# High and low parts of the samples' input rows stacked on 40 partitions: one broadcast product per sample in place of two

## The chip, the cores and the metric

The kernel runs on one core of one Trainium2 chip. The metric is the device time of one execution, in microseconds; lower is better. The comparison is between this kernel and the same kernel with the change.

## What is computed

The reference is one step of a hybrid decoder layer: an adaLN-modulated RMS norm, one input projection, a sliding-window attention branch (A), a gated linear recurrence (B, HGRN2), two merged output projections and a residual. It is done for a prompt of 2048 rows and, apart from that, for one token of each of eight samples. The change touches only one step of the samples' branch B, the update and the reading of the recurrent state (DEC_SEQ is 1, so the chunked scan has one step):

```
# per sample b and head h; S is 128 x 128 (key dim x value dim)
S_new = exp(log_f)[:, None] * S + k_in[:, None] * v[None, :]
o     = q @ S_new
```

Here v is the sample's row of the projection that the kernel calls ib, 4 heads x 128 = 512 values. The outputs are S_new of all samples and, through o, the samples' rows of y.

## The kernel before

**Tiles and stages.** The prompt is worked off in four iterations (`it` 0 to 3) of 512 rows. Each iteration is a fixed list of units (`UNITS`, NU in all): input projections of kinds B, A, za, f, qb, ib, zb, the merge gates ga and gb, the projections pa and pb, and at the end the output units `("o0", t)` and `("o1", t)` for the four row tiles. A unit is up to 24 dense products on TensorE (L717 or L720) into one of two PSUM banks, D0 and D1, which alternate. fp32 operands are split into a high part of type fp32r and a low part, and each product is done as hi x hi, hi x lo and lo x hi. ScalarE makes the high part of weights (L926) and GpSimd the low part (L1580); of the inputs h they are L942 and L1588.

**Order.** Every engine runs through the same list of units and half units, written out in Python. Small side tasks are put between the halves by the table `SIDE`, the samples' work among them. Nothing is scheduled at run time: each engine works in its own order and waits on counting semaphores. `do()` on VectorE makes an instruction increment a semaphore and then waits for it (`settle`); `s.done()` only increments. A unit can start on TensorE when its bank was emptied. For output units VectorE empties the bank in `evac` (L1310) and then adds the residual (L1312); a unit uses the bank of the unit two before it.

**The samples' states.** At the end of iteration 0, ahead of the evacuation of unit NU-3 (an output unit), VectorE runs a set-up block (L1551 to L1558). It waits for `h_lo` and `s_win`, then writes the selector `esel`, in which row b is one in the 128 columns of sample b, splits the eight rows `ibS` into `ib_hi` and `ib_lo`, signals `s_ib`, clears R3 and copies the samples' q into it, and signals `esel`. The semaphore wait on `h_lo` is there because R3 was a buffer of h.

In iteration 1 the task `vB` of sample b follows half unit (b + 1, 0). TensorE broadcasts the sample's row of 512 values to all 128 partitions of bank XD, by two products with the selector as weights:

```
mm(bank[:, :], esel[:, a, :], ib_hi, start=True, stop=False)
ins = mm(bank[:, :], esel[:, a, :], ib_lo, start=False, stop=True)
```

These are L812 and L813. GpSimd has meanwhile scaled the state (L1636), which came by DMA at the start of iteration 1, and VectorE adds the outer product from the bank, head by head (L1517). One unit later the task `so` on TensorE sums q over the new state (L818, four products per sample, one per head, and as many weight loads), which needs L1517 of that sample; the state then goes out by DMA.

Of the kernel before, what the change touches and what calls it, by code (L numbers as in the profile page):

```python
# [11 lines left out]
F32, F32R, I32, U8 = mybir.dt.float32, mybir.dt.float32r, mybir.dt.int32, mybir.dt.uint8  # L12
ALU, ACT, AX = mybir.AluOpType, mybir.ActivationFunctionType, mybir.AxisListType

D, SEQ, NS = 1024, 2048, 8
TB, NIT = 512, 4
P, KT, NT = 128, D // 128, TB // 128
# [281 lines left out]
def build(nc, A, O):  # L299

    ctx = ExitStack()
    with ctx:
        def sb(name, shape, dt=F32):
            return ctx.enter_context(nc.sbuf_tensor(name, shape, dt))


        ident, ones = sb("ident", [P, P]), sb("ones", [P, P])
# [40 lines left out]
        esel_t = sb("esel_t", [P, 1024], F32R)  # L348
# [13 lines left out]
        first = ExitStack()  # L362
        rowsS = first.enter_context(nc.sbuf_tensor("rowsS", [8, 1280], F32))
        first.close()
        rowsR = sb("rows_r", [8, 1280], F32R)
        qkS, vS, ibS = rowsS[:, 0:640], rowsS[:, 640:768], rowsS[:, 768:1280]
        ckv = R3[:, :].rearrange("p (a b n) -> p a b n", a=2, b=4)
        kTs = R2[:, 0:512].rearrange("p (b n) -> p b n", b=4)
        ps_s = kst[0:8]
        AT32 = kst[:, :, :].rearrange("p h (t i) -> p (h t) i", t=NT)  # L370
        sq_in = ibS[:, 0:256]
        esel = esel_t[0:8, :].rearrange("p (b n) -> p b n", b=NS)
        ib_hi, ib_lo = rowsR[:, 0:512], rowsR[:, 768:1280]
        qz_b = R3[:, :].rearrange("p (h b c) -> p h b c", h=HB, b=NS)
        vrow, selbc = kst[0:NV, 0], kst[:, 1]

# [22 lines left out]
        def f32(ap):  # L399
            return ap.bitcast(F32)  # L400
# [245 lines left out]
        def _(pe):  # L646
            mm, tr = nc.tensor.matmul, nc.tensor.transpose
            s = Eng(pe, "none", S)
            s.wait_ge("p_load0", 64)
            for k in range(KT):  # L650
                ins = tr(XA[:, 9 * k:9 * k + 9], R2[0:9, P * k:P * k + P], ident[0:9, 0:9])
            s.done(ins, "p_T")
            s.wait_ge("p_c", 1)
            for p in range(4):
                for k in (2 * p, 2 * p + 1):
                    s.wait_ge(f"ada{k}", 16)
                for n, b in enumerate(("D0", "D1", "XC", "XD")):
                    for k in (2 * p, 2 * p + 1):
                        r = slice(32 * (k % 4), 32 * (k % 4) + 32)
                        ins = mm(pb[b][r, :], cT[:, k, :], ada[k][:, 512 * n:512 * n + 512], start=k < 4, stop=k >= 4)  # L660
# [20 lines left out]
            for n in range(2 * KT):  # L681
                ins = mm(pb["D0"][:, 9 * n:9 * n + 9], mod_rows[:, P * n:P * n + P], sel, start=True, stop=True)
# [41 lines left out]
            def side(it, task, a, key):  # L724
# [8 lines left out]
                b = BANK[key]  # L733
                bank = pb[b]
                if PARTS[key][0] == (task, a):
                    s.wait_ge(f"{b}_free", USE[key])
                if task == "gm":
                    for p in range(4):
                        s.wait_ge(f"gw{p}", 16)
                        for n in range(2):  # L740
                            for k in (2 * p, 2 * p + 1):
                                r = slice(32 * (k % 4), 32 * (k % 4) + 32)
                                ins = mm(bank[r, 512 * n:512 * n + 512], cT[:, k, :],
                                         gate_w[p][:, k % 2, 512 * n:512 * n + 512], start=k < 4, stop=k >= 4)
                elif task == "gb":
                    s.wait_ge("grow", 1)
                    s.wait_ge("p_late", 1)
                    for n in range(2):
                        ins = mm(bank[:, 512 * n:512 * n + 512], selbc, grow[:, 512 * n:512 * n + 512],
                                 start=True, stop=True)  # L750
                elif task == "gS":
                    for k in range(KT):
                        ins = mm(bank[:, NS * k:NS * k + NS], grow[:, P * k:P * k + P], sel[:, 0:NS],
                                 start=True, stop=True)
                elif task == "bu":
                    n = it * NB + a
                    s.wait_ge("p_scale", 1)
                    s.wait_ge(f"w_in{n % NRAW}", came[n])
                    c = [b_ for _, b_ in PARTS[key]].index(a)
                    raw = w_raw[:, n % NRAW]  # L760
                    kind = BLOCKS[a][0]
                    if kind == "pa":
                        s.wait_ge("s_yb", 1)
                        s.freed(0, "sO", 1)
                        for h in range(2):
                            for k in range(4):
                                ins = mm(bank[32 * k:32 * k + 32, P * (2 * c + h):P * (2 * c + h) + P],  # L767
                                         yS[:, 4 * h + k, :], raw[:, 4 * h + k, :], start=True, stop=True)
                    else:
                        if kind == "out":  # L770
                            s.wait_ge("s_y", 4)
                        for k in range(KT):
                            ins = mm(bank[32 * (k % 4):32 * (k % 4) + 32, P * c:P * c + P], hS[:, k, :], raw[:, k, :],
                                     start=k < 4, stop=k >= 4)
# [3 lines left out]
                elif task in ("sx", "sy"):  # L778
# [4 lines left out]
                    else:  # L783
                        for c in range(nb):
                            ins = mm(bank[:, NS * c:NS * c + NS], srow[:, P * c:P * c + P], sel[:, 0:NS],  # L785
                                     start=True, stop=True)
# [22 lines left out]
                                     pTs[:, 8 * b_ + M4 * g:8 * b_ + M4 * g + M4], start=True, stop=True)  # L809
                elif task == "vB":  # L810
                    s.wait_ge("s_ib", 1)
                    mm(bank[:, :], esel[:, a, :], ib_hi, start=True, stop=False)  # L812
                    ins = mm(bank[:, :], esel[:, a, :], ib_lo, start=False, stop=True)  # L813
                elif task == "so":
                    s.freed(1, "vB", a)
                    s.wait_ge("esel", 1)
# [310 lines left out]
        def _(dve):  # L1127
# [4 lines left out]
            def do(ins, name=None):  # L1132
                s.done(ins, name)
                s.settle()
# [414 lines left out]
            for it in range(NIT):  # L1549
                for u in range(NU):  # L1550
                    if (it, u) == (0, NU - 3):  # L1551
                        s.wait_ge("h_lo", 8)
                        s.wait_ge("s_win", 32)
                        do(cp(esel, ident[0:8, 0:8].unsqueeze(2).broadcast_to([8, 8, P])))
                        do(cp(ib_hi, ibS))
                        do(tt(ib_lo, ibS, f32(ib_hi), ALU.subtract), "s_ib")
                        do(v.memset(R3[:, :], 0.0))
                        do(cp(qz_b.rearrange("p h b c -> p h (b c)")[:, :, 0:232:33], qS), "esel")  # L1558
                    for hf_ in (0, 1):
                        tasks = SIDE.get((it, u, hf_), [])  # L1560
                        early = [x_ for x_ in tasks if hf_ and x_[0] in ("PV", "norm")]
                        for task, a, _, key in early:
                            side(it, task, a, key)
                        if hf_:
                            evac(it, u)
                        for x_ in tasks:
                            if x_ not in early:
                                side(it, x_[0], x_[1], x_[3])
# [125 lines left out]
```

## Time and profile before

| What | us |
|---|---|
| median of 3 runs | 1648.69 (1648.18 to 1651.08) |
| the profiled execution | 1649.62 |
| span of its trace | 1647.8 |
| TensorE busy in the span | 1610.2 |
| VectorE busy | 763.6 |
| GpSimd busy | 830.3 |
| ScalarE busy | 594.7 |

The span is that of the instructions in the trace; the profiled execution's own time is 1.8 us longer. Times inside the trace are counted from the start of the span. Matmuls are recorded with durations that overlap, so that the distance of their starts or ends tells the rate. PE is TensorE, PEld its weight loads, DVE is VectorE, ACT ScalarE, POOL GpSimd. In a timeline, x8 means that eight equal neighbours were merged into one row, and the brackets tell how long the engine idled before the row and who released it. PEclk is the granted clock of TensorE as a share of 2.4 GHz.

### The profile page before, as it was taken

To read this page: it belongs to the slowest core of one execution; us is meant where nothing else is said; L and a number is where in the kernel's file an instruction comes from. 1 tells how busy PE (TensorE), PEld (TensorE's weight loads), DVE (VectorE), ACT (ScalarE), POOL (GpSimd) and SP (SyncE) were. 2 spreads that over 40 slices of the span, in tenths; PEclk is the share of its full clock that TensorE was granted. 3 is DMA by queue.
4 is the path that set the end of the run, shared out by engine and by line. 5 is a ranking of instruction groups with operands and counts; after the bars stand their busy time and mean duration, and the time that the engine had idled before them with its cause. 6 is when DMAs were issued, how large, how long until landed. Compare 5 with 4: busy or idle time off the path is not lost.

```text
span 1647.8 us, 31328 instructions
## 1 busy us (share of the span) xinstructions
PE 1610.2 (98%) x12840; PEld 1297.1 (79%) x12840; DVE 763.6 (46%) x1843; ACT 594.7 (36%) x1160; POOL 830.3 (50%) x1088
## 2 busy tenths in 40 slices
PE   6899999999999999999999999999999999999998
PEld 2687788877878777788878877888888977788887
DVE  2665444323558664522234764623346764633122
ACT  3335423334322551333432354243432354233330
POOL 1624433366664452446666353336677354346671
PEclk9899999999999999999999999999999999999999
DMA  8712212343545331233355232223455232123352
GB/s 315 214 53 85 70 41 65 90 128 105 173 131 131 103 90 35 71 92 114 103 168 139 54 92 63 63 69 115 128 169 162 66 89 66 54 67 88 94 164 72
DMA packets 299848, 172.62 MB, mean 105 GB/s; under 512 B 73646, under 2 KB 290055, under 8 KB 298664
## 3 DMA queue, kind: packets, MB, share of 16 engines
q1 hardware_dynamic: 299704, 170.61, 35.4%
q8 instruction: 102, 1.67, 0.4%
q14 instruction: 42, 0.34, 0.1%
HBM read 159.66 MB, written 11.96 MB: 104 GB/s over the span
## 4 chain that ended last, share of the span: by engine, by line
PE 68%; DVE 2%; issue 1%; ACT 0%; DVEq 0%
PE ps_D L720 39%; PE ps_D L717 18%; PE ps_XB L882 1%; PE ps_XB L876 1%; PE ps_XA L870 1%; PE ps_XB L848 1%; PE ps_XA L848 1%; PE ps_XB L895 1%; PE ps_XA L900 1%; PE ps_XB L894 1%; ACT p_or_hf L1064 0%; DVE p_or_hf L1416 0%; PE ps_XC L887 0%; PE ps_XC L785 0%; PE ps_XD L767 0%
## 5 line engine op out<-in xcount | busy, mean ns | idle before, releaser
L1580 POOL TENSOR_TENSOR w_lo_t<-w_raw,w_hi_t 128x256 fp32r<-128x256 f32 x928 | 680.7, 767 | 657.6 <-ACT w_hi_t L926 657.6
L720 PE MATMUL ps_D<-h_hi_t,w_hi_t 128*128 128x512 f32 x1024 | 415.1, 405 | 0.0
L720 PE MATMUL ps_D<-h_lo_t,w_hi_t 128*128 128x512 f32 x1024 | 401.1, 392 | 0.0
L720 PE MATMUL ps_D<-h_hi_t,w_lo_t 128*128 128x512 f32 x1024 | 400.1, 391 | 0.0
L926 ACT ACTIVATE w_hi_t<-w_raw 128x1024 fp32r<-128x1024 f32 x232 | 240.0, 1052 | 72.3 <-PE ps_D L717 39.3
L720 PEld LDWEIGHTS ps_D<-h_hi_t,w_hi_t 128*128 128x128 f32 x1024 | 192.3, 188 | 58.4 <-issue 21.2
L720 PEld LDWEIGHTS ps_D<-h_hi_t,w_lo_t 128*128 128x128 f32 x1024 | 192.3, 188 | 42.4
L720 PEld LDWEIGHTS ps_D<-h_lo_t,w_hi_t 128*128 128x128 f32 x1024 | 192.6, 188 | 35.8
L717 PE MATMUL ps_D<-w_hi_t,h_hi_t 128*128 128x384 f32 (+1 forms) x384 | 142.2, 370 | 2.7 <-POOL h_lo_t L1588 2.1
L717 PE MATMUL ps_D<-w_hi_t,h_lo_t 128*128 128x384 f32 (+1 forms) x384 | 136.6, 356 | 0.0
L717 PE MATMUL ps_D<-w_lo_t,h_hi_t 128*128 128x384 f32 (+1 forms) x384 | 136.6, 356 | 0.0
L717 PE MATMUL ps_D<-w_hi_t,y_hi_t 128*128 128x512 f32 x256 | 101.7, 397 | 2.1 <-DVE acc_t L1310 2.1
L717 PE MATMUL ps_D<-w_hi_t,y_lo_t 128*128 128x512 f32 x256 | 100.5, 393 | 0.0
L717 PE MATMUL ps_D<-w_lo_t,y_hi_t 128*128 128x512 f32 x256 | 100.3, 392 | 0.0
L989 ACT ACTIVATE th_t<-ps_D,bm_half 128x512 f32<-128x512 f32 x48 | 33.1, 689 | 143.5 <-PE ps_D L720 143.5
L717 PEld LDWEIGHTS ps_D<-w_hi_t,h_hi_t 128*128 128x128 f32 x384 | 72.7, 189 | 14.8 <-issue 8.4
L1292 DVE SCALAR_TENSOR_TENSOR acc_t<-th_t,ps_D 128x512 f32<-128x512 f32 x24 | 16.5, 688 | 140.5 <-PE ps_D L720 140.5
L1064 ACT ACTIVATE p_or_hf<-p_or_hf,sm 128x256 f32<-128x256 f32 x128 | 63.6, 498 | 45.6 <-DVE sm L1400 43.9
L717 PEld LDWEIGHTS ps_D<-w_lo_t,h_hi_t 128*128 128x128 f32 x384 | 72.7, 189 | 5.5
L717 PEld LDWEIGHTS ps_D<-w_hi_t,h_lo_t 128*128 128x128 f32 x384 | 72.8, 190 | 4.6
L1428 DVE SCALAR_TENSOR_TENSOR state<-state,ff,ps_XA 128x128 f32<-128x128 f32 x64 | 18.0, 343 | 117.2 <-PE ps_XA L900 117.2
L1350 DVE TENSOR_TENSOR qq<-qq,ff 128x1024 f32<-128x1024 f32 x28 | 37.6, 1345 | 72.1 <-PE ps_XB L848 45.5
(377 smaller groups left out, 2438.5 us busy)
## 6 DMA issues: line engine op xcount, KB each, us to landing
w_raw<-in_w_in SPq DMA_DIRECT2D x72, 512.0 KB, 3.9
w_raw<-in_w_merge SPq DMA_DIRECT2D x64, 512.0 KB, 4.0
w_raw<-in_w_in SPq DMA_DIRECT2D x64, 256.0 KB, 3.9
w_raw<-in_w_out SPq DMA_DIRECT2D x32, 512.0 KB, 4.1
x_or_AT<-in_x_prompt SPq DMA_DIRECT2D x20, 512.0 KB, 5.4
w_raw<-in_w_proj_a SPq DMA_DIRECT2D x64, 128.0 KB, 2.9
w_raw<-in_w_proj_b SPq DMA_DIRECT2D x32, 256.0 KB, 3.2
xr<-in_x_prompt SPq DMA_DIRECT2D x16, 512.0 KB, 5.1
```

The lines of the kernel that those rows point to most:

```text
L717: ins = mm(bank[:, 0:P * nb].rearrange("p (n c) -> p n c", c=P), a[:, k, P * j:P * j + P], w[:, s0:s0 + nb, k, :], start=go, stop=end)
L720: ins = mm(bank[:, :], w[:, s0, k0 + k, :], a[:, k, :], start=go, stop=end)
L848: ins = mm(bank[32 * g:32 * g + left, m * n:m * n + m], kk[:, h, c + 32 * g:c + 32 * g + left], right, start=True, stop=True)
L870: ins = mm(bank[i:i + 32, c:c + 160], qT[r, 2 * mp + m, P * t + i:P * t + i + 32], kT[r, P * t + i:P * t + i + 160], start=True, stop=True)
L876: ins = tr(bank[:, 512 * kt + P * m:512 * kt + P * m + P], p_t[:, m, P * kt:P * kt + P], ident[:, :])
L926: s.done(fn(w_hi[:, SLOT[n % NB]], w_raw[:, n % NRAW], ACT.Copy), "w_hi")
L989: s.leave(fn(dst, bank[:, :], ACT.Tanh, scale=0.5, bias=bm_half[:, c:c + 1]), it, u)
L1064: fn(p_t[:, m, :], p_t[:, m, :], ACT.Exp, bias=negm[:, m:m + 1], accum_out=rsum[:, m:m + 1])
L1292: leave(stt(acc[:, :], thx("ga", j), 1.0, bank[:, :], ALU.add, ALU.mult), it, u)
L1350: s.done(tt(qr, qr, fl[:, :, :, 0:1].broadcast_to(shape), ALU.mult))
L1428: ins = stt(state[:, h, :], state[:, h, :], ff[:, h, P * a:P * a + 1], bank[:, P * h:P * h + P], ALU.mult, ALU.add)
L1580: ins = g_.tensor_tensor(w_lo[:, c, k:k + 2], w_raw[:, n % NRAW, k:k + 2], f32(w_hi[:, c, k:k + 2]), ALU.subtract)
```

## The change

The two parts of the samples' rows are stacked in one tile of 40 partitions: the high part in rows 0 to 7, the low part in rows 32 to 39, zeros in rows 8 to 31. The selector has its ones in rows 0 to 7 and again in rows 32 to 39, and is zero in rows 8 to 31. One product over 40 rows then adds up both parts. Its operands are written by more instructions in the set-up block: the selector by a copy of 32 rows and one of 8 rows, the zeros by a multiplication of 32 x 512 by 0.0, which reads the identity matrix. The low part is now written to other partitions than it is read from.

```diff
-        rowsR = sb("rows_r", [8, 1280], F32R)
+        rowsR = sb("rows_r", [40, 1280], F32R)
...
-        esel = esel_t[0:8, :].rearrange("p (b n) -> p b n", b=NS)
-        ib_hi, ib_lo = rowsR[:, 0:512], rowsR[:, 768:1280]
+        esel = esel_t[0:40, :].rearrange("p (b n) -> p b n", b=NS)
+        ib2 = rowsR[:, 0:512]
...
                     s.wait_ge("s_ib", 1)
-                    mm(bank[:, :], esel[:, a, :], ib_hi, start=True, stop=False)
-                    ins = mm(bank[:, :], esel[:, a, :], ib_lo, start=False, stop=True)
+                    ins = mm(bank[:, :], esel[:, a, :], ib2, start=True, stop=True)
...
-                        do(cp(esel, ident[0:8, 0:8].unsqueeze(2).broadcast_to([8, 8, P])))
-                        do(cp(ib_hi, ibS))
-                        do(tt(ib_lo, ibS, f32(ib_hi), ALU.subtract), "s_ib")
+                        for r in (slice(0, 32), slice(32, 40)):
+                            s.done(cp(esel[r], ident[r, r.start:r.start + 8].unsqueeze(2).broadcast_to([r.stop - r.start, 8, P])))
+                        do(ts(ib2[0:32].rearrange("p (n c) -> p n c", c=P), ident[0:32].unsqueeze(1).broadcast_to([32, 4, P]),
+                              0.0, None, ALU.mult))
+                        do(cp(ib2[0:8], ibS))
+                        do(tt(ib2[32:40], ibS, f32(ib2[0:8]), ALU.subtract), "s_ib")
```

## Rows read from the trace of the kernel before

**Rows 1.** The page: busy us (share of the span) of the engines.
```profile
PE 1610.2 (98%) x12840; PEld 1297.1 (79%) x12840; DVE 763.6 (46%) x1843; ACT 594.7 (36%) x1160; POOL 830.3 (50%) x1088
```

**Rows 2.** List of waits, TensorE: for whom; us in total, times, longest.
```profile
PE ps_XC L822 <- DVE srow L1527: 2.4, 1, 2.4
PE ps_D L717 <- DVE acc_t L1310: 2.1, 1, 2.1
```

**Rows 3.** Timeline of VectorE: start, us, line, operation.
```profile
474.37 1.15 DVE L1554 CAST esel_t<-ident 8x1024 fp32r<-8x1024 f32 x1 [4.10 <-issue]
475.55 0.84 DVE L1555 CAST rows_r<-rowsS 8x512 fp32r<-8x512 f32 x1
476.43 1.11 DVE L1556 TENSOR_TENSOR rows_r<-rowsS,rows_r 8x512 fp32r<-8x512 f32 x1
477.82 0.91 DVE L1557 MEMSET PT_or_qa<- 128x1024 f32 x1 [0.28 <-DVE rows_r L1556]
...
479.00 0.69 DVE L1310 TENSOR_TENSOR acc_t<-ps_D,gate_bc 128x512 f32<-128x512 f32 x1
...
487.22 0.69 DVE L1310 TENSOR_TENSOR acc_t<-ps_D,gate_bc 128x512 f32<-128x512 f32 x1 [4.99 <-PE ps_D L717]
```

**Rows 4.** Timeline of GpSimd.
```profile
474.23 7.13 POOL L1580 TENSOR_TENSOR w_lo_t<-w_raw,w_hi_t 128x256 fp32r<-128x256 f32 x8
```

**Rows 5.** Timeline of TensorE at the end of iteration 0.
```profile
477.06 0.39 PE L717 MATMUL ps_D<-w_hi_t,y_lo_t 128*128 128x512 f32 x1
477.28 0.39 PE L717 MATMUL ps_D<-w_lo_t,y_hi_t 128*128 128x512 f32 x1
479.75 0.50 PE L717 MATMUL ps_D<-w_hi_t,y_hi_t 128*128 128x512 f32 x1 [2.08 <-DVE acc_t L1310]
...
480.84 0.63 PE L717 MATMUL ps_D<-w_hi_t,y_lo_t 128*128 128x512 f32 x1
481.26 0.63 PE L717 MATMUL ps_D<-w_lo_t,y_hi_t 128*128 128x512 f32 x1
```

**Rows 6.** Chain of work that ended last: start, us.
```profile
474.37 1.16 DVE esel_t L1554
...
479.00 0.70 DVE acc_t L1310
```

**Rows 7.** Windows, TensorE: window, length, busy, granted clock, DMA.
```profile
480.50:484.00 3.50, 3.50 (x10) 0.53 0.68 179
...
678.50:682.00 3.50, 2.15 (x10) 1.00 0.47 141
...
47.00:50.50 3.50, 1.44 (x6) 0.50 1.02 405
```

**Rows 8.** Line L813: durations in ns, min/median/max, first and last start.
```profile
L813 PE MATMUL ps_XD<-rows_r,esel_t x8: 387/392/393, 493.6 to 535.1; 8*128 8x512 f32 x8
```

**Rows 9.** Timeline of TensorE, the pair of sample 0.
```profile
493.31 0.49 PE L812 MATMUL ps_XD<-rows_r,esel_t 8*128 8x512 f32 x1
493.65 0.39 PE L813 MATMUL ps_XD<-rows_r,esel_t 8*128 8x512 f32 x1
493.97 0.44 PE L717 MATMUL ps_D<-w_hi_t,h_hi_t 128*128 128x384 f32 x1
```

**Rows 10.** Timelines of TensorE and its weight loads at the state sums.
```profile
499.31 0.43 PE L818 MATMUL ps_XC<-s_st_hi,PT_or_qa 128*32 128x128 f32 x8 [0.78 <-issue]
...
504.81 0.16 PEld L818 LDWEIGHTS ps_XC<-s_st_hi,PT_or_qa 128*32 128x32 f32 x8 [0.23 <-DVE s_st_hi L1517]
...
516.10 0.42 PE L818 MATMUL ps_XC<-s_st_hi,PT_or_qa 128*32 128x128 f32 x8 [0.20 <-DVE s_st_hi L1517]
```

**Rows 11.** Lines L1251, L1365 and L1476 of VectorE, ns as above.
```profile
L1251 DVE TENSOR_SCALAR kk<-th_t,k_scale,k_bias x16: 534/744/962, 143.9 to 1364.0; 128x512 f32<-128x512 f32 x16
...
L1365 DVE COPY x_or_AT<-kst_t x16: 415/418/973, 251.1 to 1440.9; 32x512 f32<-32x512 f32 x16
...
L1476 DVE COPY rowsS<-ps_XC x1: 678/678/678, 203.4 to 203.4; 8x512 f32<-8x512 f32 x1
```

## The prediction

> **What bounds the kernel now.** Start with the page's busy shares: TensorE is busy 98% of the span, VectorE 46%, GpSimd 50% [rows 1]. So a removed product is worth its time on TensorE, and work added to another engine is free unless TensorE comes to wait for it. The next view to read is therefore the list of TensorE's waits [rows 2]: outside the start-up there are only a few, and one of 2.1 us, behind only one of 2.4, is for VectorE's L1310, the evacuation of an output unit. That one lies exactly at the code that the change lengthens.
>
> The VectorE timeline shows why [rows 3]. The set-up block (L1554 to L1558) is put ahead of the evacuation of unit NU-3. It starts at 474.37, after 4.1 us of idling, because it waits for GpSimd's last low part of h; GpSimd goes on to its next work (L1580) at 474.23 [rows 4], so that is when this part was done. The block's last large instruction is L1557 at 477.82, 0.91 us, then a copy of 32 columns (L1558), and only then comes L1310 at 479.00. On TensorE [rows 5] the last product of unit NU-2 starts at 477.28, and the first of NU-1 at 479.75, 2.08 us idle, released by that L1310: NU-1 needs the bank which NU-3 filled. The chain of work that ended last goes through the block and then L1310, 0.70 us from 479.00 [rows 6], into TensorE. So the block has no cover at all at its end: each microsecond added to it delays TensorE by one. What lay under it before (the end of unit NU-2) is already used up.
>
> The clock is the third thing to see. In the stretch right after the gap the granted clock is 0.53 on average (480.5 to 484.0) [rows 7]. The products there start 0.42 us apart (480.84, 481.26) instead of 0.22 (477.06, 477.28) [rows 5]: the lower level of 1.2 GHz in place of 2.4. With 0.53 over 3.5 us, about 3.3 us were at half speed, so it cost some 3.5 x 0.47 = 1.6 us.
>
> **The change, part by part.** *Removed: one of two products for each of eight samples.* L812 and L813 are 8 rows x 512 columns, 0.49 us [rows 9] and 0.39 us [rows 8] as recorded. Recorded durations overlap; what counts is the distance. The starts go 493.31 (L812), 493.65 (L813), 493.97 (next L717) [rows 9], so by starts one product is 0.32 to 0.34 us. By ends (start plus duration) it is 493.80 to 494.04, 0.24 us, close to the 0.22 us of the dense 512-column products in [rows 5]. The other 0.1 us sits in the recorded duration of the first product (0.49 against 0.39) and ahead of the dense product behind the pair: what a change of shape costs at the two edges, which stay. I take 0.235 each: 8 x 0.235 = 1.9 us; by starts it would be 8 x 0.33 = 2.7. The Trainium skill (TensorEngine Tiling (Array Packing), Key Properties) says that a change of the tiling mode drains TensorE; by that rule the drains lie before L812 and before the dense product, none between L812 and L813, and the removal gives 1.9, while the distance of starts gives 2.7.
>
> Not all of it arrives. Each state sum L818 needs VectorE's L1517 of the sample before. For sample 0 TensorE idled 0.78 us before 499.31 [rows 10]; that state comes by DMA through GpSimd's L1636, which no product of this pair speeds up, so reaching this point 0.23 us earlier only lengthens the wait. For sample 1 the weight load at 504.81 idled 0.23 us and for sample 3 the product at 516.10 idled 0.20, both for L1517 [rows 10], which stands behind VectorE's other work. So the savings of samples 0, 1 and 2 are partly or wholly lost, those of 3 to 7 are kept: 5 x 0.235 = 1.2 at least, 8 x 0.235 = 1.9 if none is lost. I take six, 1.4 us.
>
> *The one product that stays* has 40 rows in place of 8. The trace has no 40-row product, so it lies between 8 rows and 128 rows. Those with 512 columns are recorded at 0.39 us for 8 rows [rows 8] and 0.39 us for 128 rows [rows 5]: nothing, and both bounds are the same.
>
> *Added: the selector copy a second time.* The copy into rows 0 to 31 has the same 1024 elements per partition as L1554, and another follows into rows 32 to 39. From the start of L1554 to that of L1555 is 1.18 us [rows 3]. Whether 8 or 32 partitions are written doesn't matter (an evacuation of 8x512, L1476, takes 0.68 us [rows 11], and one of 128x512, L1310, 0.69 [rows 3]). So +1.18 us.
>
> *Added: the zero fill* of 32 x 512 by a multiplication with 0.0. Nearest rows: the VectorE scaling L1251 of 512 elements, 0.74 us at the median, 0.53 to 0.96 at the ends; the cheapest 512-element copy of 32 partitions, L1365, is 0.42 [rows 11]. GpSimd works through the whole block (eight pieces in 7.13 us without a gap [rows 4]), and the block's own copy of 512 elements, L1555, took 0.85, twice the cheapest of that length. I take 0.72, bounds 0.42 and 0.96. The copy of the high part and the subtraction for the low part remain, 0.85 and 1.11 us [rows 3]; that the latter now writes to partition 32 changes only which rows it writes. The two may come out differently beside GpSimd's work, as 0.42 against 0.85 for 512 elements shows; as only part of that is left to vary, I allow 0.3 upward and downward for both.
>
> Sum for the block: 1.18 + 0.72 = **+1.9 us** (1.3 to 2.5), all of it ahead of L1310 and so all on TensorE. The gap grows from 2.1 to 4.0 us, with TensorE starting again at about 481.65. The other work behind the block is the evacuation of NU-2 and the store of output rows; VectorE idles 4.99 us after that [rows 3], which takes up the lateness. GpSimd's and ScalarE's splits of weights wait for TensorE here, so they are shifted by as much and make no new wait.
>
> *The clock.* If the lower level lies where it lay, until about 484, TensorE now spends only 484.0 - 481.65 = 2.35 us of it working at half speed: it loses 1.2 instead of 1.6, so -0.4 us. If the longer gap makes a second such stretch follow, that adds 1.6: +1.2 us. Both are possible by the rows: here the low stretch ended with TensorE busy throughout it, and from 47.0 to 50.5, where TensorE was busy 1.44 us only, the clock was at 0.50 [rows 7]. And the wait of 2.4 us for L1527 [rows 2] brought no fall: the stretch in which it ended (678.5 to 682.0, TensorE busy 2.15 us of 3.5) has 1.00 [rows 7]. So the fall depends on where the gap lies, and can be absent in some executions of the kernel before. I take the middle of -0.4 and +1.2, +0.4. The Trainium skill (TensorE: Matmul & The Clock Gate, Why this matters for your kernels) advises against idle gaps between bursts of products because they bring back the low clock; by this advice the change is the wrong trade, and the +1.2 holds.
>
> **Sum:** +1.9 - 1.4 + 0.4 = +0.9 us. The profiled execution took 1649.62 us (span 1647.8 and 1.8 around it); so about 1650.5 for one like it. The median of the runs, 1648.69, lies 0.93 below it, and on the median the same difference gives **1649.6 us**. A measurement of this kernel can tell about 0.2%, 3.3 us, from no change, so this is "the same".
>
> **Rivals.** *Slower: the clock.* If the median execution before has no low stretch (it is 0.9 us faster than the profiled one, which had one), and the 4 us gap makes two each time, the clock costs 1.2 + 1.6 = 2.8 and the whole is 1.9 - 1.4 + 2.8 = +3.3; with the block at its upper bound of 2.5 it is +3.9: 1652.6. It decides against "the same" once clock and block together pass 4.7 us (3.3 + 1.4). For it: the median below the profiled time. Against it: the clock has to be at its worst in the one kernel and at its best in the other. Chance 0.12.
>
> *Faster: the products count fully and the block is cheap.* 2.7 saved by starts, block 1.3, clock -0.4: 1.3 - 2.7 - 0.4 = -1.8 us, 1646.9. Even that is inside 0.2%; to be faster than 3.3 us the block would have to be hidden besides, against which speaks that TensorE waits for it now. Chance of over 0.2% faster 0.03.
>
> *The saving doesn't come at all.* If TensorE runs into VectorE or a DMA later in the iteration and gives the 1.4 back, the cost of the block stands alone: +1.9 + 0.4 = +2.3, 1651.0. For it: the three waits of [rows 10]. Against it: in the later iterations TensorE has hardly any waits; the longest is the 2.4 us of [rows 2]. Chance 0.15, within 0.2% too.
>
> The likeliest, a net of -0.5 to +2.0 us, has 0.70. The range: from the fast rival to the slow one, 1646.9 to 1652.6. Faster 0.03, same 0.85, slower 0.12.
>
> **What would show each step.** In the profile after: eight products of 40x512 in place of sixteen of 8x512, with about 0.42 us from its start to that of the next dense product; a new copy of about 1.15 us and a scaling of 0.4 to 1.0 us in the block; L1310 of NU-3 at about 480.9 and a TensorE wait for it of about 4.0 us; a low clock until 484 or until 487.5; waits at the state sums of samples 0, 1 and 3 a little longer. I am wrong if the block's additions are hidden (the wait stays 2.1), if the 40-row product takes longer than the pair's 0.66, or if the clock stays low for longer than two such stretches.

## The result: 3.9 us slower

The changed kernel takes 1654.27 us (median of 20 runs, 1651.41 to 1658.12), the kernel before 1650.37 us beside it (20 runs, 1648.18 to 1653.49). The ratio is 1.0023, with a 95% interval of 1.0016 to 1.0030. In a second comparison on another chip it was 1.0033 (1.0021 to 1.0045). So it is slower, by 0.23%: outside the stated range, and slower by over 0.2%, which had a chance of 0.12. The median of before has itself moved up by 1.7 us from the three runs that the prediction went by; the difference to it is 3.9 us, not the 5.6 that a subtraction from 1648.69 would give. Taken as a difference, 3.9 us is just the upper end of the range. All ratios are of fast runs; one execution of 3196.42 us, among the twelve of the last kernel below (lateso_pad), isn't in its ratio.

The profiled executions differ by 5.4 us in their spans (1653.2 against 1647.8). First TensorE's waits in the changed kernel, from 465 to 655; L1309, L817, L875 and L847 are L1310, L818, L876 and L848 of before:

```profile
PE ps_D L717 <- DVE acc_t L1309: 4.6, 1, 4.6
...
PE ps_XA L847 <- issue: 1.0, 1, 1.0
PE ps_XB L875 <- DVE p_or_hf L1415: 0.6, 2, 0.3
PE ps_XC L817 <- DVE s_st_lo L1516: 0.5, 1, 0.5
```

The wait for the evacuation is 4.6 us in place of 2.1 [rows 2]. The next three rows are what a median can't show: the waits of 1.0 and 0.5 us have no counterpart of before in this stretch, and L875 has two waits where it had one. The waits for sample 0's and sample 3's states are 1.1 and 0.4 us, in place of 0.8 and 0.2. The VectorE timeline of the changed kernel at the block:

```profile
474.29 2.30 DVE L1554 CAST esel_t<-ident 32x1024 fp32r<-32x1024 f32 x2 [4.08 <-issue]
476.63 0.84 DVE L1555 TENSOR_SCALAR rows_r<-ident 32x512 fp32r<-32x512 f32 x1
477.51 0.83 DVE L1557 CAST rows_r<-rowsS 8x512 fp32r<-8x512 f32 x1
478.37 1.09 DVE L1558 TENSOR_TENSOR rows_r<-rowsS,rows_r 8x512 fp32r<-8x512 f32 x1
479.74 0.91 DVE L1559 MEMSET PT_or_qa<- 128x1024 f32 x1 [0.28 <-DVE rows_r L1558]
480.69 0.78 DVE L1560 COPY PT_or_qa<-smS 128x32 f32<-128x32 f32 x1
481.50 0.69 DVE L1309 TENSOR_TENSOR acc_t<-ps_D,gate_bc 128x512 f32<-128x512 f32 x1
```

Against [rows 3]: two selector copies, 2.30 us for both (predicted 2.3); the zero fill 0.84 (predicted 0.72); the two splits 0.83 and 1.09, as they were. The surprise is the last instruction, the copy of 32 columns of q (L1560): 0.78 us. The same copy took 0.20 us before, and was small enough to be passed over in the prediction:

```profile
478.77 0.20 DVE L1558 COPY PT_or_qa<-smS 128x32 f32<-128x32 f32 x1
```

From the start of the block to L1309 it is 7.21 us in place of 4.63: +2.6, just over the prediction's upper bound of 2.5.

GpSimd's splits of weights run through the whole block in both kernels. Before it is [rows 4]; in the changed kernel:

```profile
474.16 7.25 POOL L1582 TENSOR_TENSOR w_lo_t<-w_raw,w_hi_t 128x256 fp32r<-128x256 f32 x8
```

So GpSimd's presence alone doesn't make the copy of q slow. In all fourteen profiles of this study a split runs beside this copy. It took 0.20 us in eight of them and 0.78 in six, and these six are the ones whose block was lengthened at its place. In the six it ends 0.05 us after the end of a GpSimd piece that started within 0.01 us of it. What decides seems to be how the two engines fall against each other; no run here forces that.

Windows of TensorE (window, length, busy, granted clock, DMA):

```profile
479.50:482.00 2.50, 0.00 (x0) 0.58 0.00 0
482.00:487.00 5.00, 4.75 (x12) 0.53 0.69 174
487.00:490.00 3.00, 3.00 (x15) 1.00 1.17 305
684.50:688.50 4.00, 4.00 (x13) 0.57 0.02 4
```

The low clock (0.5, the 1.2 GHz level) now covers two stretches' worth, from about 480 to 486.7, in place of the one of [rows 7]. And it falls a second time at 684.7, behind the 2.4 us wait for L1526, where the kernel before had 1.00. Now TensorE's timeline at four places, the gap, the start of iteration 1, the product of sample 0 and the first dense product after that of sample 7:

```profile
477.23 0.39 PE L717 MATMUL ps_D<-w_lo_t,y_hi_t 128*128 128x512 f32 x1
482.25 0.79 PE L717 MATMUL ps_D<-w_hi_t,y_hi_t 128*128 128x512 f32 x1 [4.63 <-DVE acc_t L1309]
...
489.90 0.33 PE L717 MATMUL ps_D<-w_hi_t,h_hi_t 128*128 128x384 f32 x1
...
496.26 0.50 PE L812 MATMUL ps_XD<-rows_r,esel_t 40*128 40x512 f32 x1
496.69 0.44 PE L717 MATMUL ps_D<-w_hi_t,h_hi_t 128*128 128x384 f32 x1
...
537.15 0.50 PE L720 MATMUL ps_D<-h_hi_t,w_hi_t 128*128 128x512 f32 x1
```

and the rows of before that answer to the third and the last, which are not among the rows read before:

```profile
486.95 0.33 PE L717 MATMUL ps_D<-w_hi_t,h_hi_t 128*128 128x384 f32 x1
...
535.40 0.51 PE L720 MATMUL ps_D<-h_hi_t,w_hi_t 128*128 128x512 f32 x1
```

Iteration 1 starts 2.95 us later (489.90 against 486.95). After sample 7's product the lag is 1.75 (537.15 against 535.40): the eight products did save 1.2 us there. From the start of the 40-row product to that of the dense one is 0.43 us, in place of 0.66 for the pair [rows 9]. So to this point all is as forecast, in kind. But the lag doesn't stay at 1.75. It is 5.4 at the end. The 3.6 us in between, and the 2.95 of the start, are what the experiments are about.

### The profile page after: what moved, and what is told of

Its sections match the earlier page's. It is cut to its first block, busy times and chain, and to the rows that moved or that the text cites. A ratio compares the mean times of both kernels' runs of the same rounds, so it can differ in the third digit from the quotient of the medians.

```text
span 1653.2 us, 31314 instructions
## 1 busy us (share of the span) xinstructions
PE 1612.0 (98%) x12832; PEld 1297.9 (79%) x12832; DVE 764.9 (46%) x1845; ACT 594.5 (36%) x1160; POOL 831.5 (50%) x1088
## 4 chain that ended last, share of the span: by engine, by line
PE 66%; DVE 4%; issue 1%; ACT 1%; POOL 0%; DVEq 0%; POOLq 0%
PE ps_D L720 38%; PE ps_D L717 17%; PE ps_XB L881 1%; PE ps_XB L875 1%; PE ps_XA L869 1%; PE ps_XB L847 1%; PE ps_XA L847 1%; PE ps_XA L899 1%; PE ps_XB L894 1%; PE ps_XB L893 1%; ACT p_or_hf L1063 1%; DVE p_or_hf L1415 0%; POOL w_lo_t L1582 0%; PE ps_XC L886 0%; PE ps_XC L785 0%
## 5 line engine op out<-in xcount | busy, mean ns | idle before, releaser
L717 PE MATMUL ps_D<-w_hi_t,h_hi_t 128*128 128x384 f32 (+1 forms) x384 | 141.9, 369 | 2.7 <-POOL h_lo_t L1590 2.1
L717 PE MATMUL ps_D<-w_hi_t,h_lo_t 128*128 128x384 f32 (+1 forms) x384 | 136.4, 355 | 0.0
L717 PE MATMUL ps_D<-w_lo_t,h_hi_t 128*128 128x384 f32 (+1 forms) x384 | 136.3, 355 | 0.0
L717 PE MATMUL ps_D<-w_hi_t,y_hi_t 128*128 128x512 f32 x256 | 102.1, 399 | 4.6 <-DVE acc_t L1309 4.6
L717 PE MATMUL ps_D<-w_hi_t,y_lo_t 128*128 128x512 f32 x256 | 100.5, 393 | 0.0
L717 PE MATMUL ps_D<-w_lo_t,y_hi_t 128*128 128x512 f32 x256 | 100.4, 392 | 0.0
L717 PEld LDWEIGHTS ps_D<-w_hi_t,h_hi_t 128*128 128x128 f32 x384 | 72.7, 189 | 13.9 <-issue 7.6
L717 PEld LDWEIGHTS ps_D<-w_lo_t,h_hi_t 128*128 128x128 f32 x384 | 72.5, 189 | 5.5
L717 PEld LDWEIGHTS ps_D<-w_hi_t,h_lo_t 128*128 128x128 f32 x384 | 72.7, 189 | 4.6
```

What stands on the lines that cost most here:

```text
L717: ins = mm(bank[:, 0:P * nb].rearrange("p (n c) -> p n c", c=P), a[:, k, P * j:P * j + P], w[:, s0:s0 + nb, k, :], start=go, stop=end)
```

## Experiments

All ratios are to the kernel before on the same chip. long_two, cheap_one, early_two and early_one shared one chip and 27 runs of before (median 1648.28). before_again, after_again, pad_one and early_pad shared another and 28 runs (1649.73). pad_front and the three lateso kernels shared a third and 35 runs (1648.62). A ratio's interval is about 0.1%, 1.6 us, to either side, so the medians alone don't tell two kernels apart that differ by less than some 2 us.

**1. The block alone: long_two.** Two products as before, with the block of the change.

```diff
-                        do(cp(esel, ident[0:8, 0:8].unsqueeze(2).broadcast_to([8, 8, P])))
+                        for r in (slice(0, 32), slice(32, 40)):
+                            s.done(cp(esel40[r], ident[r, r.start:r.start + 8]...))
+                        do(ts(rowsR[0:32, 0:512]..., ident[0:32]..., 0.0, None, ALU.mult))
                         do(cp(ib_hi, ibS))
```

> The kernel before with its two products of 8 rows, and the set-up block lengthened by the instructions that the change adds (selector copied to 32 and to 8 rows, zero fill of 32 x 512), at their place. 'Place': block 2.2 to 2.6 us longer, all of it in TensorE's gap, and a low clock of 6.8 instead of 3.4 us: 3 us more by unit 0 of iteration 1, 3 to 5 us over the kernel before at the end; slower than the changed kernel by 1 to 2. 'Later': less than 2 us over the kernel before, as the product is unchanged.

1651.97 us, ratio 1.0026 (1.0016 to 1.0036): +3.7 us at the medians. TensorE's wait at the evacuation (L718 and L1311 are L717 and L1310 of before):

```profile
PE ps_D L718 <- DVE acc_t L1311: 4.6, 1, 4.6
```

Its profile is its slowest run (1656.41 us), with two more low stretches, from 506 and from 687. In it iteration 1 starts at 491.96, 5.0 us later than before; 1.7 of this is there since the start-up, so 3.3 us belong to the block and the clock behind it.

The block by itself, with the clock that follows it, costs about all that the change costs: theory "place" had the block right. But by it the changed kernel, which has the saving of the products besides, should be 1 to 2 us faster than this one. Its ratios, 1.0023 and 1.0033, don't show that.

**2. The product with a shorter block: cheap_one.** The selector in one instruction, the zeros in the start-up.

```diff
-                        for r in (slice(0, 32), slice(32, 40)):
-                            s.done(cp(esel[r], ...))
-                        do(ts(ib2[0:32]..., ident[0:32]..., 0.0, None, ALU.mult))
+                        e1, e2 = (ident[0:40, c:c + 8].unsqueeze(2).broadcast_to([40, 8, P]) for c in (0, 32))
+                        do(tt(esel, e1, e2, ALU.add))
```

> The changed kernel with one product per sample, its block shortened at its place: the selector written by one addition of two parts of the identity over 40 partitions (1.2 to 1.4 us in place of 2.3), the zero fill done once in the start-up where VectorE is idle. 'Place': the block is about as long as before (4.7 us), TensorE's gap 2.2 us, and the gain of the products is seen alone: 1 to 2 us under the kernel before. 'Later': not faster than the kernel before.

1651.72 us, ratio 1.0026 (1.0014 to 1.0037). Missed: it isn't faster than before. Half of the miss is the block, which came out longer than meant:

```profile
475.81 1.69 DVE L1556 TENSOR_TENSOR esel_t<-ident 40x1024 fp32r<-40x1024 f32 x1 [4.10 <-issue]
...
480.75 0.77 DVE L1560 COPY PT_or_qa<-smS 128x32 f32<-128x32 f32 x1
```

The addition with two inputs in SBUF took 1.69 us for the 1024 elements that a copy does in 1.15, and the copy of q again 0.77. TensorE's gap was 3.2 us, so 1.1 over the kernel before and not 0.1. The rest is not in the gap. In the profile 1.3 us are saved by the end of sample 7's product, 1.7 given back by 655, and 1.6 lost at a fall of the clock at 683. Over the runs the mean granted clock is 0.9915, against 0.9929 for before: 0.0014 of 1650 us is 2.3 us.

**3. The set-up moved: early_two and early_one.** The same instructions, but the selector and the rows are written in VectorE's idle time ahead of the wait for the last low part of h.

```diff
-                        s.wait_ge("h_lo", 8)
+                        s.wait_ge("h_lo", 7)
                         s.wait_ge("s_win", 32)
                         ...
+                        s.wait_ge("h_lo", 8)
                         do(v.memset(R3[:, :], 0.0))
```

> The kernel before (two products, its own shorter set-up) with the same move of the set-up ahead of the wait. 'Place': minus 2.1 and minus 1.6, about 3.7 us under the kernel before, and 1.4 to 1.9 us over the one-product kernel with the same move. 'Later': the same as or faster than the one-product kernel with the move.

> The changed kernel with the same instructions, but the writing of the selector and of the stacked rows stands ahead of the wait for the last low part of h (it waits only for the third of the four tiles), in the idle time that VectorE had before the block; the clearing of R3 and the copy of q stay behind the wait. Theory 'place' (what the change costs is the length of the block ahead of the evacuation L1310, with the clock that falls after TensorE's gap; the product itself is a gain): the evacuation comes at about 477 instead of 481.5, TensorE's gap disappears, no low clock follows there, and the time is that of the kernel before minus 2.1 (gap) minus 1.6 (clock) minus 1.4 to 1.9 (products): about 5 us under the kernel before. Rival 'later' (the 40-row product, or what comes after it in iteration 1, costs a good part): not more than 2 us under the kernel before, and TensorE waits of over 1 us in all between 535 and 650.

With two products 1647.08 us, ratio 0.9990 (0.9981 to 0.9999); with one 1649.12, ratio 1.0005 (0.9996 to 1.0013). The VectorE timeline with two products:

```profile
470.31 1.20 DVE L1554 CAST esel_t<-ident 8x1024 fp32r<-8x1024 f32 x1
...
475.26 0.91 DVE L1558 MEMSET PT_or_qa<- 128x1024 f32 x1 [1.64 <-POOL h_lo_t L1589]
...
476.64 0.69 DVE L1310 TENSOR_TENSOR acc_t<-ps_D,gate_bc 128x512 f32<-128x512 f32 x1 [0.24 <-DVE PT_or_qa L1559]
```

The block begins at 470.31 in place of 474.37, and the evacuation comes at 476.64, before TensorE needs it: the 2.1 us wait is gone from the list. As theory "place" had it. In this profile the whole gain is there: iteration 1 starts at 482.93 in place of 486.95, and TensorE is still 3.8 us ahead at 655. But it is the fastest of the eleven runs (1644.03 us, granted clock 0.996). Their median is only 1.2 us under before and their mean 2.0, with a mean granted clock of 0.9932 against 0.9929. So most runs must have their low clock at some other place, which the one kept trace of this kernel doesn't show.

And the kernel with one product is *slower* than that with two, by 2.0 us at the medians on the same chip. That is the rival's forecast: "later" had the two-product kernel the same or faster, and for the one-product kernel waits of over 1 us between 535 and 650, of which the profile shows 1.5. So each theory was right on one part, "place" on the block and "later" on the products. The pair leaves the block out nearly altogether: in the profiles iteration 1 starts 0.3 us later with one product. Not all of the 2.0 us is waiting, though. early_one's profile has a low clock from 497, behind a wait of 1.5 us for sample 0's state, while in early_two's that wait is 1.1 us and the clock stays up. The mean granted clocks are 0.9924 and 0.9932, which is some 1.3 us.

**4. Twice the same kernels: before_again and after_again.** A second profile of each, to see which stalls belong to the program.

> The kernel before, unchanged, as a second profile and as a control on this chip. If the stalls in the traces are of the program and not of the execution, it has again no TensorE wait in the state sum of sample 7, in the first transpose of the probabilities after it, or in the small products of the level at 642, and a gap of 2.1 us at 479.75. The clock falls may lie elsewhere. Ratio 1.000.

> The changed kernel, unchanged, as a second profile and for a ratio on this chip beside the others. 'Program': the three stalls of the one-product kernels (0.5 at sample 7, 0.4 behind it, 1.0 in the level products, 1.9 us in all) are there again, and the time is about 4 us over the kernel before. 'Execution': they are at other places or missing.

1649.84 us (ratio 1.0004, 0.9994 to 1.0014) and 1653.99 (1.0033, 1.0021 to 1.0045). The second profile of the changed kernel has the stalls at the same places, 0.5 at sample 7's state sum and 0.5 in the level products, and that of the kernel before has neither. Over all profiles of this study: the five with one product and no padding have the stall in this batch of level products, the five with two products don't. In a later batch, at 1410 to 1420, it is otherwise: there the kernel before stalls as well, 0.7 us in its first profile and 1.1 in its second.

**Where the saving goes: VectorE meets GpSimd.** VectorE in the changed kernel ahead of sample 7's state sum, and GpSimd at that time:

```profile
541.68 0.18 DVE L1154 TENSOR_SCALAR sm<-sm 128x24 f32<-128x24 f32 x1
541.89 0.71 DVE L1155 TENSOR_TENSOR sm<-sm 128x24 f32<-128x24 f32 x1
542.64 0.65 DVE L1379 TENSOR_SCALAR sm<-sm 128x24 f32<-128x24 f32 x1
543.21 1.11 DVE L1516 SCALAR_TENSOR_TENSOR s_st_lo<-ps_XD,smS,s_st_lo 128x128 f32<-128x128 f32 x4
...
541.83 2.80 POOL L1582 TENSOR_TENSOR w_lo_t<-w_raw,w_hi_t 128x256 fp32r<-128x256 f32 x4 [3.11 <-ACT w_hi_t L925]
```

and before:

```profile
539.66 0.18 DVE L1156 TENSOR_TENSOR sm<-sm 128x24 f32<-128x24 f32 x1
539.88 0.18 DVE L1380 TENSOR_SCALAR sm<-sm 128x24 f32<-128x24 f32 x1
539.97 1.12 DVE L1517 SCALAR_TENSOR_TENSOR s_st_lo<-ps_XD,smS,s_st_lo 128x128 f32<-128x128 f32 x4
...
540.09 2.81 POOL L1580 TENSOR_TENSOR w_lo_t<-w_raw,w_hi_t 128x256 fp32r<-128x256 f32 x4 [3.31 <-ACT w_hi_t L926]
```

These are the last steps of a chain of small instructions (the reciprocal square root of the queries' norms). They take 0.18 us each, and 0.71 and 0.65 when GpSimd's split of the next weights runs beside them; a GpSimd piece is 0.70 us (four in 2.80). Before, the split begins at 540.09, when VectorE is already at L1517, which takes 1.12 us with and without it. GpSimd's split comes 1.74 us later than before, VectorE's step at 541.89 comes 2.23 us later than the same one at 539.66. GpSimd's split follows TensorE, by way of ScalarE, and profits from the saved time. This VectorE chain is paced by its own work and profits less, and so the two meet. VectorE then is 1 us late, TensorE waits 0.5 for it at once and is 0.4 behind at the next place (L875).

That a split slows such instructions can be counted. In the fourteen traces 4176 small instructions of VectorE on the tile `sm` (1 to 24 columns) ran with no split beside them, and none took more than 0.19 us. Another 1066 started while a piece of a split was under way; 79% of them took over 0.4 us, and these ended 0.02 to 0.04 us after the end of a piece.

**And TensorE stalls in the level products.**

```profile
643.61 1.20 PE L847 MATMUL ps_XA<-qq,kk 128*32 128x16 f32 x120
645.81 0.26 PE L847 MATMUL ps_XA<-qq,kk 128*32 128x16 f32 x8 [1.00 <-issue]
...
q8 instruction: 1, 0.02, 2.2%
```

The level's 128 small products are broken off after 120, for 1.0 us, and no semaphore is waited for there. In the kernel before this batch (at 641.05) runs through. The last row is of the window 643.0 to 645.5. It shows one load of the queue q8, of 16 KB, which began at 643.36 and was over at 644.23, before the stall. q8 is read here as the queue that loads TensorE's instructions, since it has 102 such loads for TensorE's 25,680 instructions.

**5. Padding: pad_one and pad_front.** A product of 2 columns ahead of each broadcast product, or all eight of them ahead of the first.

```diff
+                    mm(bank[:, 0:2], esel[:, a, :], ib2[:, 0:2], start=True, stop=True)
                     ins = mm(bank[:, :], esel[:, a, :], ib2, start=True, stop=True)
```

> The changed kernel with a product of 2 columns ahead of each of the eight broadcast products, so that TensorE's instruction stream is as long as in the kernel before. Theory 'fetch': the 1.0 us stall inside the level's small products (120 of them, stall, 8) comes from where the blocks of 256 instructions of TensorE's stream begin, which eight products less have shifted; with the padding it disappears, while the stalls for VectorE at sample 7 and behind it stay. The padding costs 0.06 to 0.15 us each, 0.5 to 1.2 in all, so the time is about that of the changed kernel or up to 1 us less. Rival 'VectorE': the level's stall is a consequence of VectorE's lateness in iteration 1 and stays.

> The changed kernel with the eight products of 2 columns all ahead of sample 0's broadcast product, so that TensorE's stream is as long as before behind this point, but TensorE gains its full 0.23 us per sample on VectorE. 'Fetch and lead are two causes': the stall inside the level's products at about 645 is gone, and the two stalls for VectorE, 0.5 at sample 7's state sum and 0.4 behind it, are there. 'One cause (padding slowed TensorE down enough)': all three are there. 'One cause (the stream)': all three are gone. Time 1 to 2 us under the changed kernel in the first case.

pad_one, 1650.90 us, ratio 1.0011 (1.0001 to 1.0022), is 3.1 us under the changed kernel on the same chip (2.2 by the means), though it does more; at most 1 us was expected. Its wait for the evacuation is still 4.6 us, but the level products run through, and the two VectorE stalls, which were expected to stay, are gone as well:

```profile
643.86 1.27 PE L848 MATMUL ps_XA<-qq,kk 128*32 128x16 f32 x128
```

That spoke for the length of the stream; pad_front speaks against it. Its stream is as long from sample 0 on, and it has all three stalls; the level products now stop after 112 in place of 120. Ratio 1.0020 (1.0012 to 1.0029), 1652.05 us.

```profile
PE ps_XA L849 <- issue: 0.9, 1, 0.9
PE ps_XC L819 <- DVE s_st_lo L1518: 0.5, 1, 0.5
```

So it was the outcome "one cause (padding slowed TensorE down enough)" as far as VectorE's stalls go. The eight padding products (16 instructions with their weight loads) move the place where the level products break by eight products, as a boundary of instruction blocks would move. Whether TensorE stalls there is another question: pad_one and the kernel before have this boundary too and don't stall. "Fetch" in its simple form, that the length of the stream decides, has fallen.

The traces do show what goes with the stall: a late load. In the six profiles that stall in this batch, a load of q8 begins 0.25 to 0.72 us before the batch does. In the eight that don't, the load begins 4.3 to 4.9 us before it and is over at least 3.3 us ahead of it. The eight other stalls of level batches, all at 1410 to 1420, have such a load too, 0.15 to 0.81 us before their batch. But a late load is not enough: six other batches, of the 336 with all 128 products, had one and ran through. Why the load comes late in some kernels is not known, and no run forces it.

**6. The versions that give the lead something to do: early_pad, lateso_two, lateso_one.** early_pad is early_one with pad_one's padding. The lateso kernels have the moved set-up and each state sum half a unit later on TensorE:

```diff
-            put(1, _b + 2, 0, "so", _b, "XC", (1, "so", 0))
+            put(1, _b + 2, 1, "so", _b, "XC", (1, "so", 0))
```

> The changed kernel with the set-up moved ahead of the wait for the last low part of h (as in the first of the experiments) and the same padding. 'Fetch': the level's stall of 0.8 to 1.0 us is gone, and the time is 0 to 1 us under the moved kernel without padding. 'VectorE': the stall stays, and the time is 0.5 to 1 us over it.

> The kernel before with the set-up moved into VectorE's idle time, and each state sum of iteration 1 half a unit (about 2.6 us) later on TensorE. In the moved kernels TensorE arrives early at sample 0's state sum and waits 1.1 to 1.9 us for the state; if this wait is where the move's gain of 3.7 us was given back, it is gone here, with no low clock at 497, and the time is 3 to 4 us under the kernel before. If the gain goes somewhere else, it is 1 to 2 us under it, as without this.

> The same with one product of 40 rows per sample and no padding. TensorE's waits at the state sums of samples 0, 1, 3 and 7 are gone, the stall in the level's products may be there (0.8 to 1.0). If the merged product is worth its 0.23 us per sample once nothing else waits: 1.9 us under the two-product version without that stall, 1 us under it with the stall. If VectorE collides with GpSimd all the same, no gain over the two-product version.

early_pad 1647.87 us, ratio 0.9987 (0.9978 to 0.9997), the fastest measured beside early_two, and without the stall in the level products, as "fetch" had it; lateso_two 1648.05, ratio 0.9993 (0.9984 to 1.0001); lateso_one 1648.36, ratio 0.9996 (0.9986 to 1.0006). The two lateso kernels missed their numbers: putting off the state sums didn't bring the move's gain back. The last, lateso_pad, is lateso_one with the padding:

> The same with one product of 40 rows and a product of 2 columns ahead of it, which keeps the stream's length: no stall in the level's products, a saving of 0.12 us per sample, 1 us in all, against the two-product version: 4 to 5 us under the kernel before.

It gave 1648.02, ratio 0.9994 (0.9985 to 1.0002), and missed its 4 to 5 us as well. One thing that takes the gain is seen in early_pad, at sample 0's state sum and in the window after it:

```profile
496.68 0.43 PE L818 MATMUL ps_XC<-s_st_hi,PT_or_qa 128*32 128x128 f32 x8 [1.87 <-issue]
...
498.00:501.50 3.50, 3.50 (x13) 0.51 1.29 254
```

TensorE arrives 1.9 us too early for the state that comes by DMA (0.78 before [rows 10]), and the clock falls behind this wait, to 0.51 for 3.5 us. Against pad_one, which differs only by the move, early_pad is 7.2 us ahead at the start of iteration 1 and 4.7 behind this place, so 2.6 us are lost here. The same fall is in all four profiles with the move and one product, and in neither of the two with the move and two products. In the lateso kernels the wait is only renamed: 1.0 us (two products) and 1.6 us (one) at the broadcast product of the next sample, for the same outer product (L1517, L1516). And lateso_one has no stall for VectorE at sample 7, but the one in the level products is there (0.7 us): the two are separate.

## Why the prediction was wrong, step by step

*The place of the block: right.* Every added microsecond went into TensorE's wait (2.1 to 4.6, long_two 4.6), and long_two shows that it costs 3.7 us (2.6 to 5.9 by the interval) with all that follows.

*"Sum for the block: +1.9 us (1.3 to 2.5)": too small.* It was 2.6. (The bounds of the terms add up to 2.4, not 2.5: 1.18 + 0.96 + 0.3.) The selector was right (1.15), the zero fill 0.84 in place of 0.72, and 0.58 came from the copy of q behind them, 0.78 in place of 0.20. I had listed it as a small thing at the end. The allowance of 0.3 us for timing against GpSimd was for the two splits only, which came out as they were; the instruction that did change was not in the sum.

*"The clock, +0.4": too small by half.* The step took the middle between one low stretch and two. All five profiles with a wait of 4.6 or 4.7 us have two, but the first of them begins in the gap, where a low clock costs nothing. From TensorE's restart until iteration 1 the lag grew from 2.5 (482.25 against 479.75) to 2.95, so by 0.45. In the four other profiles it grew by 0.8 to 1.1, each against the kernel before's first profile. For the place itself the term is 0.4 too small in the mean of the five, and its closeness in the first profile is luck. Over the runs the mean granted clock is 0.9916 in the changed kernel (20 runs), 0.9913 in its second comparison against 0.9925 for before (28 runs) on that chip; 0.0012 of 1650 us is 2.0 us, some of it idle time. The profile of the changed kernel had the additional fall at 684.7 too, its second profile did not. The rival "slower: the clock" gave +3.9 and had 0.12. That its amount is the measured one is partly luck: it put 2.8 us on the clock and kept the saving of 1.4.

*"Not all of it arrives ... I take six, 1.4 us": the size was right up to sample 7, but the step took it for kept. This is the step that failed.* 1.2 us arrived behind sample 7, and then 0.5, 0.4 and 1.0 were given back, 1.9 in all. In the second profile 1.3 us arrived and 1.1 went back. This is the rival "the saving doesn't come at all" (chance 0.15). Against it I had held that TensorE hardly waits later. That is a list of the waits at the old pace; it doesn't tell how near VectorE was. In the pair early_one and early_two, where the block plays nearly no part, one product is 2.0 us slower than two, some 1.3 of it by the clock.

*The 40-row product costs what the 8-row product does: right,* 0.50 us recorded against 0.49, and the distance 0.43 as forecast (0.42). The drain rule from the Trainium skill (TensorEngine Tiling (Array Packing), Key Properties), by which a product inside a pair saves 0.235 and not 0.33 us, was on the right side here: 0.66 - 0.43 = 0.23. So was the advice of the Trainium skill (TensorE: Matmul & The Clock Gate, Why this matters for your kernels) against idle gaps between bursts: the gap of 4.6 us was followed by two low stretches, 6.8 us, in place of one.

*The verdict.* Two of the cases that I had kept as rivals of the likeliest occurred together, and the range had each of them only by itself. Together they are, in the profile: 2.95 until iteration 1 - 1.2 + 1.9 given back = 3.65, and 4 x 0.43 = 1.7 for the fall of the clock at 684.7 (4 us at 0.57), which makes 5.4, the difference of the spans. The fall at 684.7 belongs to the execution more than to the kernel: it is in eight of the fourteen profiles, the kernel before's second among them.

*A part outside the trace.* The execution's time is 1.8 us (1.7 to 1.9) over the span of its instructions in every run whose span is recorded of the kernel before, and of the kernels with two products or with padding. In the changed kernel it is up to 3.0, in the mean 2.3 (20 runs) and 2.4 (6 runs); cheap_one, early_one and lateso_one have such runs too, up to 2.9. So some 0.4 to 0.6 us of the loss lies where no trace looks. The prediction had carried the 1.8 us over unchanged.

*What stays open.* Why the load of instructions comes late in some of the kernels with the boundary in the level products and not in the others, and whether it is what stops TensorE. What the time outside the span is, and why only the kernels with one product and no padding have more of it. Why pad_one is so much faster than the changed kernel: of the 2.2 us between their means 0.6 lie outside the span, and the 1.6 inside it are still more than the 1.1 to 1.9 us given back in the changed kernel's two profiles less what the padding costs; the intervals allow it. And that VectorE's lateness at sample 7 is GpSimd's doing was seen in the traces that have it and lack it, and in the count above, but not forced by an experiment on GpSimd.

## What to carry to other kernels

Ask of a saving on the bounding engine who paces the others: VectorE and GpSimd here are started by TensorE at one place and by a DMA or by each other at the next, and in the traces a shift of half a microsecond between them made two meet that had just missed each other. Set-up work for a later stage belongs into an idle stretch ahead of the wait that it doesn't need; moving three instructions ahead of one semaphore wait (early_two) gave 1.2 us at the medians (0.2 to 3.1), and the merged products gave nothing. A single profile is one execution: early_two's was the fastest of eleven, long_two's the slowest of nine, and both would mislead without the other runs' times and clocks. And a prediction whose rivals can come together needs the range of their sum.

## What the runs showed of the hardware that was not expected

- Small VectorE instructions on SBUF took mostly 0.65 to 0.78 us instead of 0.18 to 0.20 when they started while a piece of a GpSimd split (0.70 us) was under way, and ended just after such a piece (79% of 1066 over 0.4 us; none of 4176 without a split beside them over 0.19). The copy of 32 columns of q shows that it need not be: beside the same splits it took 0.20 us in eight profiles and 0.78 in six. The slow copy cost nearly as much as the fill of 512 columns (0.84).
- An addition of two broadcast views of SBUF took 1.69 us for 40x1024 beside GpSimd's work; the copy of one such view took 1.12 to 1.20 us for 1024 elements with 8 or 32 partitions, beside it too.
- TensorE can stall 0.5 to 1.1 us inside a batch of small products without a semaphore. All 14 such stalls in the fourteen traces followed a load of q8 that began 0.15 to 0.81 us before the batch. The place moved by eight products when eight were added ahead.
- After a wait of 2.4 us (L822 and its like) the clock fell in eight profiles and stayed up in six, and two profiles of one kernel could differ: a fall at 684.7 in the changed kernel's first and none in its second, none in before's first and one at 679.9 in its second. After 4.6 or 4.7 us of waiting it was low for 6.8 us in all five profiles, after 2.1 or 3.2 us for 3.4 in all three.
